# Expert layers of a streaming encoder: one gathered, sorted token table, windows copied per expert, and the scatter moved between the next gate-up matmuls

## The chip, the cores and the metric

One Trainium2 chip, one core. The metric is the device time of one launch in microseconds, the median of several runs. TensorE's clock has two levels, 1.2 and 2.4 GHz; the profile gives the granted share, 0.50 or 1.00, as PEclk.

## The reference, cut to what matters

One step of a two-layer encoder over 320 tokens (256 of a prompt, 64 of a sample). Layer 0 mixes with RWKV-7, layer 1 with windowed attention; both end in the same hierarchical mixture of experts, which is what the change touches. There are 32 experts in 4 groups; each token takes one group and two experts of it. All is float32.

```python
gu  = jnp.einsum('sd,edf->sef', t, w_gu)            # t: tokens x 1024, w_gu: 32 x 1024 x 512
hid = jax.nn.silu(gu[..., :D_EXPERT]) * gu[..., D_EXPERT:] * cw[..., None]   # D_EXPERT = 256
return jnp.einsum('sef,efd->sd', hid, w_down)       # w_down: 32 x 256 x 1024
```

`cw` is zero for every expert that a token didn't choose, so only the chosen rows need computing. A layer's expert weights are 32 x 3 MiB, 100.7 MB, all of which must come from device memory.

## The kernel before

The program is one block per engine with hand-placed semaphores. TensorE's `mm` (line 664) issues nearly all matmuls, so nearly all bear that line.

**Ahead of the expert loop** (`moe`, TensorE line 938, ScalarE 1292, VectorE 1615): mean square and normalisation (`rms`, line 1450), with the clearing of `ysum` (line 1618) between the coefficients and `rms`; router logits; the tokens turned to rows (`htok`) and split by ScalarE, GpSimd and VectorE into three bf16 parts whose sum is the float32 value (`hpart`); routing on VectorE; a rank matmul that numbers each expert's tokens (`posn`); and the number of passes, 64 slots per expert and pass.

**The expert loop** does four experts a turn, in two pairs (u = 0, 1), eight turns a pass. A pair fills the 128 rows, 64 slots for each expert:

- VectorE `select` (1719) compares `posn` with 1 to 64 and gives the one-hot matrix `sel`.
- TensorE `gather` (971): 8 chunks x 3 token tiles x 3 parts = 72 bf16 matmuls a pair, `hpart` as weights and `sel` with 128 columns as moving operand. ScalarE `gathered` (1314) copies the result to `xe`.
- TensorE turns `sel` (into `selT`) and picks the slot weights (`cwpart`).
- Gate-up, float32, 512 columns; ScalarE's SiLU (1327); VectorE's product with the slot weight (1740); `hid_turn` (985), VectorE's copy (1746); `down` (995) into banks 4 and 5.
- ScalarE, VectorE and for the first pair GpSimd (`low_parts`, 607) split the result in three bf16 parts, `dpart` (lines 1333, 1753, 1337, 1757, 618).
- The scatter: 8 chunks x 6 bf16 matmuls of 320 columns, `dpart` against `selT`; VectorE adds each chunk to `ysum` (1762).

TensorE's order in a turn is written by hand (`experts`, 1010): the selector work of both pairs, gate-up of both, first `hid_turn`, gather of the next turn's pair 0, second `hid_turn`, both `down`, gather of the next turn's pair 1, scatter. The loop is entered with both gathers of turn 0.

**The loads** are all on SyncE's queue (`moe_loads`, 485). The ring has four slots, each holding one expert's gate-up (2 MiB) and down weights (1 MiB). The slots of the first four experts are filled before the loop. In the loop, `again` (504) waits for gate-up of pair 0, issues two gate-up loads, the same for pair 1, then two down loads behind each pair's `down`.

Of the kernel before, what the change touches and what calls it, by code (L numbers as in the profile page):

```python
# [36 lines left out]
P = 128  # L37
# [19 lines left out]
TILES = [(0, 128), (128, 128), (256, 64)]  # L57
SEQS = [(0, 0, SEQ), (1, SEQ, DEC)]
# [35 lines left out]
def constants():  # L94
# [46 lines left out]
    return {"const_all": c, "const_wkv": w, "const_att": a}  # L141
# [93 lines left out]
def build(nc, i, o, known, seen):  # L235
    ctx = ExitStack()
    with ctx:
# [3 lines left out]
        def sem(name):  # L241
# [28 lines left out]
        in_sems = {n: sem(n) for n in ("const_in", "vec_in", "x_in", "wkvc_in", "attc_in", "sink_in", "cache_in",  # L270
# [3 lines left out]
            "pos_ready", "sel_ready", "selT_made", "selT_ready", "xe_made", "xe_ready",  # L274
# [51 lines left out]


        hpart = wk(3 * 3 * D // 2, BF16).rearrange("p (s j d) -> p s j d", s=3, j=3)
        ysum = wk(B).rearrange("p (c t) -> p c t", c=C)
        htok = work[:, off[0]:off[0] + 3 * D].rearrange("p (j d) -> p j d", j=3)  # L330
        xe = wk(2 * C * P).rearrange("p (u c s) -> p u c s", u=2, c=C)

        dpart = wk(3 * D, BF16).rearrange("p (u s d) -> p u s d", u=2, s=3)
        rest = wk(D).rearrange("p (n d) -> p n d", n=2)
# [4 lines left out]
        selT = wk(T, BF16).rearrange("p (u t) -> p u t", u=2)  # L339
        lg = wk(3 * 36).rearrange("p (j n) -> p j n", j=3)  # L340
# [8 lines left out]
        g48 = wk(3 * 4 * 8).rearrange("p (j g e) -> p j g e", j=3, g=4)  # L349

# [219 lines left out]
        def _(eng):  # L570
# [61 lines left out]
            eng.dma_start(cph[:, 0:AN], i["const_att"]).then_inc(in_sems["attc_in"], 16)  # L632
            split_rows(0)
# [24 lines left out]
        def _(eng):  # L658
# [279 lines left out]
            def moe(l):  # L938
# [25 lines left out]
                pe.wait("parts", l)  # L964
                pe.wait("passes", l)
# [5 lines left out]
                def gather(k, u):  # L971

                    eng.wait_ge(S["sel_ready"], 2 * k + u + 1)
                    for hf in range(2):
                        if u == 1:
                            eng.wait_ge(S["xe_ready"], 4 * k + hf + 1)
                        for cc in range(4):
                            c = 4 * hf + cc
                            for j, (t0, kt) in enumerate(TILES):
                                for n in range(3):  # L980
                                    ins = mm(ps[1 + hf][:, P * cc:P * cc + P], hpart[0:kt, n, j, P * c:P * c + P],
                                             sel[0:kt, u, j, :], j == 0 and n == 0, j == 2 and n == 2)
                        ins.then_inc(S["xe_made"], 1)

                def hid_turn(k, u):
                    eng.wait_ge(S["h_ready"], 2 * k + u + 1)
                    if u == 0:
                        eng.wait_ge(S["y_added"], 8 * k + 1)
                    else:
                        eng.wait_ge(S["hT_ready"], 2 * k + 1)  # L990
                    for f in range(2):
                        ins = eng.transpose(ps[0][:, P * f:P * f + P], hid[:, u, P * f:P * f + P], ident)  # L992
                    ins.then_inc(S["hT_made"], 1)

                def down(k, u):
                    eng.wait_ge(S["hT_ready"], 2 * k + u + 1)
                    for v in range(2):
                        eng.wait_ge(S[f"dn_in{2 * u + v}"], 16 * k + 16)
                    for n in range(2):
# [10 lines left out]
                def experts(k, e, ahead):  # L1010

                    for u in range(2):
                        eng.wait_ge(S["xe_ready"], 4 * k + 3 + u)
                        for j, (t0, kt) in enumerate(TILES):
                            mm(ps[1 + u][:, t0:t0 + kt], sel[0:kt, u, j, :], ident16[0:kt, 0:kt], True, True)

                        for j, (t0, kt) in enumerate(TILES):
                            ins = mm(ps[1 + u][:, T:T + 6].rearrange("p (s v) -> p s v", s=3), sel[0:kt, u, j, :],
                                     cwpart[0:kt, :, j, bass.ds(e + 2 * u, 2)], j == 0, j == 2)
                        ins.then_inc(S["selT_made"], 1)  # L1020
                    for u in range(2):
                        for v in range(2):
                            eng.wait_ge(S[f"gu_in{2 * u + v}"], 16 * k + 16)
                        if u == 0:
                            eng.wait_ge(S["y_added"], 8 * k)
                        for c in range(C):
                            for v in range(2):
                                ins = mm(ps[3 + 4 * u][64 * v:64 * v + 64, :], xe[:, u, c, 64 * v:64 * v + 64],
                                         w512(2 * u + v)[:, c, :], c == 0, c == C - 1)
                        ins.then_inc(S["gu_made"], 1)  # L1030
                    hid_turn(k, 0)
                    eng.wait_ge(S["selT_ready"], 2 * k + 2)
                    if ahead:
                        gather(k + 1, 0)
                    hid_turn(k, 1)
                    down(k, 0)
                    down(k, 1)
                    if ahead:
                        gather(k + 1, 1)
                    eng.wait_ge(S["hT_ready"], 2 * k + 2)  # L1040
                    for c in range(C):
                        pb = ps[(6, 7, 3, 0)[c % 4]]
# [10 lines left out]

                with eng.Fori(0, nb) as p:
                    for u in range(2):
                        gather(8 * p, u)
                    with eng.Fori(0, EXP // 4 - 1) as k_:
                        experts(8 * p + k_, 4 * k_, True)
                    experts(8 * p + 7, EXP - 4, False)
# [104 lines left out]
        def _(eng):  # L1164
# [127 lines left out]
            def moe(l):  # L1292
# [15 lines left out]
                for j, (t0, k) in enumerate(TILES):  # L1308
                    ac.wait("rest", l, j)
                    act(hpart[0:k, 1, j, :], htok[0:k, j, :], ACT.Copy, ("middle", l, j))  # L1310
                ac.wait("passes", l)
                nb = eng.value_load(passes[0:1, 2 * l:2 * l + 1], min_val=1, max_val=5)

                def gathered(k, u):
                    for hf in range(2):
                        eng.wait_ge(S["xe_made"], 4 * k + 2 * u + hf + 1)
                        eng.activation(xe[:, u, 4 * hf:4 * hf + 4, :],  # L1317
                                       ps[1 + hf][:, :].rearrange("p (c s) -> p c s", c=4),
                                       ACT.Copy).then_inc(S["xe_ready"], 1)

                def experts(k, ahead):
                    for u in range(2):
                        eng.wait_ge(S["w_ready"], 4 * k + 2 * u + 2)
                        eng.activation(selT[:, u, :], ps[1 + u][:, 0:T], ACT.Copy).then_inc(S["selT_ready"], 1)
# [3 lines left out]
                    if ahead:  # L1328
                        gathered(k + 1, 0)
                    for u in range(2):  # L1330
                        for n in range(2):
                            eng.wait_ge(S["down_made"], 4 * k + 2 * u + n + 1)
                            eng.activation(dpart[:, u, 0, 512 * n:512 * n + 512], ps[4 + n][:, :],  # L1333
                                           ACT.Copy).then_inc(S["hi_ready"], 1)
                        for n in range(2):
                            eng.wait_ge(S["rest_ready"], 4 * k + 2 * u + n + 1)
                            eng.activation(dpart[:, u, 1, 512 * n:512 * n + 512], rest[:, n, :],  # L1337
                                           ACT.Copy).then_inc(S["mid_ready"], 1)
                    if ahead:
                        gathered(k + 1, 1)  # L1340

                with eng.Fori(0, nb) as p:
                    for u in range(2):
                        gathered(8 * p, u)
                    with eng.Fori(0, EXP // 4 - 1) as k_:
                        experts(8 * p + k_, True)
                    experts(8 * p + 7, False)
# [56 lines left out]
        def _(eng):  # L1404
# [210 lines left out]
            def moe(l):  # L1615
                S = moe_sems[l]
                coefficients(f"B{l}", vcol("norm_g", 16 * l + 8, C))
                op(eng.memset(ysum[:, :, :], 0.0))
                rms(f"B{l}")
# [84 lines left out]
                op(eng.tensor_reduce(small[:, 0:1], pb[:, 96:96 + EXP], AX.X, ALU.max), ("read", "rank", l))  # L1704
                ve.settle()

# [7 lines left out]
                ve.settle()  # L1714
                eng.memset(small[:, 8:9], 0.0).then_inc(S["pos_ready"], 1)
# [3 lines left out]
                def select(e, u):  # L1719

                    for v in range(2):
                        for j, (t0, kt) in enumerate(TILES):
                            a = slice(64 * v, 64 * v + 64)
                            ins = eng.tensor_scalar(sel[0:kt, u, j, a], cst("iota", kt),
                                                    posn[0:kt, j, bass.ds(e + v, 1)], None, ALU.is_equal, ALU.bypass)
# [154 lines left out]
```

## Time and profile before

| what | value |
|---|---|
| device time, median of 3 runs | 1529.16 us (1525.72 to 1533.57) |
| the profiled execution, first to last instruction | 1526.5 us |
| TensorE matmul busy | 1355.7 us, 89% |
| VectorE busy | 521.2 us, 34% |
| ScalarE busy | 361.9 us, 24% |
| GpSimd busy | 68.4 us, 4% |
| from HBM | 293.7 MB, 194 GB/s over the span |
| gate-up loads in the page | 64, that is 32 a layer: one pass each |

A busy share over the whole span mixes stages with different limits. The two expert loops, from about 603 to 913 us and from about 1174 to 1483 us, are stages of their own and have to be read by themselves. A matmul's busy time in the rows overlaps with its neighbours', so a count times its mean is more than the time it takes; windows and timelines give the time.

### The profile page before, as it was taken

Reading aid. Unit: us, or ns where it says so; the run is one execution under the profiler, and the core shown is the slowest. Engines: PE = TensorE matmul, PEld = TensorE weight load, DVE = VectorE, ACT = ScalarE, POOL = GpSimd, SP = SyncE. Lnnn points to the kernel's source line nnn. Section 1 sums busy time; section 2 is a strip of 40 time slices with the busy share of each in tenths; the row PEclk is TensorE's granted clock in tenths of the full one; section 3 lists DMA queues with packets and bytes.
Section 4 is the critical chain, followed back from the end, with each engine's and each line's share of the span. In section 5 each row is a group of like instructions: output and inputs, shape, how many; then the busy total and the mean of one; then the engine's idle time right before and its main releaser. Section 6 shows DMA issues by size and latency. Waiting matters only on the chain.

```text
span 1526.5 us, 27571 instructions
## 1 busy us (share of the span) xinstructions
PE 1355.7 (89%) x11807; PEld 822.6 (54%) x11807; DVE 521.2 (34%) x1268; ACT 361.9 (24%) x664; POOL 68.4 (4%) x77
## 2 busy tenths in 40 slices
PE   5699998888888968999999996987968999999994
PEld 2257665565675655554444444656755555444443
DVE  2503553333312452332223235143262333222324
ACT  1131301110122022222222222134132222222212
POOL 2000000000000010000000000000010000000000
PEclk9799989998999875999999997996965999999997
DMA  9333216766734320888888845050220888888830
GB/s 272 92 111 120 100 62 244 285 234 237 276 113 165 111 83 1 331 324 299 305 304 299 305 186 184 11 205 17 83 83 1 331 330 320 302 307 298 302 121 34
DMA packets 111383, 297.16 MB, mean 195 GB/s; under 512 B 5924, under 2 KB 7304, under 8 KB 104136
## 3 DMA queue, kind: packets, MB, share of 16 engines
q1 hardware_dynamic: 109248, 289.78, 51.7%
q0 software_dynamic: 1856, 6.15, 1.7%
q8 instruction: 64, 1.05, 0.3%
q10 hardware_dynamic: 200, 0.06, 0.0%
q14 instruction: 15, 0.12, 0.0%
HBM read 293.73 MB, written 2.24 MB: 194 GB/s over the span
## 4 chain that ended last, share of the span: by engine, by line
PE 81%; DMA 8%; DVE 7%; ACT 2%; issue 1%; SPq 0%; DVEq 0%; POOL 0%; ACTq 0%; POOLq 0%
PE bank L664 79%; DMA ring<-in_ada_w 7%; DVE work L1415 3%; DMA ring<-in_kv_ada_w 1%; ACT work L1173 1%; PE bank L992 1%; DVE x_res L1421 1%; DVE work L1418 1%; DVE rstd L1453 1%; DVE att L1814 0%; PE bank L1159 0%; PE bank L1129 0%; PE bank L682 0%; SPq L450 0%; DVE work L1421 0%
## 5 line engine op out<-in xcount | busy, mean ns | idle before, releaser
L664 PE MATMUL bank<-work 128*128 128x128 bf16 (+6 forms) x3936 | 385.2, 255 | 20.0 <-ACT work L1173 7.4
L664 PEld LDWEIGHTS bank<-work 128*128 128x128 bf16 (+2 forms) x3936 | 282.1, 110 | 132.5 <-issue 30.6
L664 PE MATMUL bank<-ring,work 128*64 128x512 f32 (+1 forms) x1760 | 351.4, 553 | 1.5 <-DVE ring L1415 1.5
L664 PE MATMUL bank<-work,ring 128*128 128x320 f32 (+4 forms) x1600 | 298.9, 362 | 11.5 <-DVE work L1418 7.0
L664 PEld LDWEIGHTS bank<-work,ring 128*128 128x128 f32 (+3 forms) x1600 | 215.7, 171 | 96.2 <-issue 23.9
L664 PEld LDWEIGHTS bank<-ring,work 128*64 128x64 f32 (+1 forms) x1760 | 116.9, 138 | 214.1 <-issue 193.5
L664 PE MATMUL bank<-ring 64*64 64x64 f32 (+2 forms) x2624 | 110.7, 231 | 5.0 <-issue 5.0
L664 PEld LDWEIGHTS bank<-ring 64*64 64x64 f32 (+2 forms) x2624 | 97.5, 143 | 31.3 <-issue 25.1
L1173 ACT ACTIVATE work<-bank 64x512 f32<-64x512 f32 (+7 forms) x110 | 52.9, 528 | 226.1 <-PE bank L664 176.9
L664 PE MATMUL bank<-ring,cs 128*32 128x512 f32 x448 | 64.7, 671 | 38.6 <-DMA ring<-in_ada_w 34.4
L1762 DVE TENSOR_TENSOR work<-work,bank 128x320 f32<-128x320 f32 x128 | 62.4, 487 | 95.3 <-PE bank L664 95.3
L1173 ACT ACTIVATE ring<-bank 128x512 f32<-128x512 f32 (+4 forms) x66 | 37.3, 564 | 189.7 <-PE bank L664 188.8
L664 PE MATMUL bank<-work,const 128*128 128x320 f32 (+2 forms) x164 | 50.9, 475 | 30.1 <-DVE work L1690 17.4
L1317 ACT ACTIVATE work<-bank 128x512 f32<-128x512 f32 x64 | 38.2, 598 | 147.2 <-PE bank L664 147.2
L1753 DVE TENSOR_TENSOR work<-bank,work 128x512 f32<-128x512 f32 x64 | 44.3, 692 | 82.5 <-ACT work L1333 82.5
L618 POOL TENSOR_TENSOR work<-work 128x512 bf16<-128x512 f32 x32 | 36.4, 1159 | 648.0 <-ACT work L1337 648.0
L1746 DVE COPY work<-bank 128x256 f32<-128x256 f32 x32 | 13.6, 424 | 145.5 <-PE bank L992 145.5
L1415 DVE TENSOR_TENSOR ring<-ring,bank 128x512 f32<-128x512 f32 x45 | 29.1, 684 | 83.8 <-PE bank L664 83.7
L1327 ACT ACTIVATE work<-bank 128x256 f32<-128x256 f32 x32 | 12.3, 384 | 189.2 <-PE bank L664 189.2
L664 PEld LDWEIGHTS bank<-work,const 128*128 128x128 f32 (+1 forms) x164 | 30.4, 214 | 49.5 <-DVE work L1690 18.2
L1740 DVE SCALAR_TENSOR_TENSOR work<-work,small,bank 128x256 f32<-128x256 f32 x32 | 15.2, 475 | 120.2 <-ACT work L1327 120.2
L1333 ACT ACTIVATE work<-bank 128x512 bf16<-128x512 f32 x64 | 37.9, 593 | 62.8 <-PE bank L664 62.8
(167 smaller groups left out, 879.9 us busy)
## 6 DMA issues: line engine op xcount, KB each, us to landing
ring<-in_moe_w_gu SPq DMA_DIRECT2D x64, 2048.0 KB, 12.9
ring<-in_moe_w_down SPq DMA_DIRECT2D x64, 1024.0 KB, 12.3
ring<-in_ada_w SPq DMA_DIRECT2D x40, 1024.0 KB, 5.1
ring<-in_rw_w_rkv SPq DMA_DIRECT2D x6, 2048.0 KB, 8.0
ring<-in_ada_w SPq DMA_DIRECT2D x4, 2048.0 KB, 31.5
ring<-in_kv_ada_w SPq DMA_DIRECT2D x8, 1024.0 KB, 5.0
ring<-in_rw_w_o SPq DMA_DIRECT2D x2, 2048.0 KB, 11.7
ring<-in_at_w_q SPq DMA_DIRECT2D x2, 2048.0 KB, 14.8
```

What stands on the lines that cost most here:

```text
L618: eng.tensor_tensor(dpart[:, 0, 2, cols], rest[:, n, :], dpart[:, 0, 1, cols], ALU.subtract).then_inc(S["lo_ready0"], 1)
L664: return eng.matmul(out, l, r, start=start, stop=stop, **kw)
L992: ins = eng.transpose(ps[0][:, P * f:P * f + P], hid[:, u, P * f:P * f + P], ident)
L1173: ac.did(eng.activation(out, in_, f, **kw), *keys)
L1317: eng.activation(xe[:, u, 4 * hf:4 * hf + 4, :], ps[1 + hf][:, :].rearrange("p (c s) -> p c s", c=4), ACT.Copy).then_inc(S["xe_ready"], 1)
L1333: eng.activation(dpart[:, u, 0, 512 * n:512 * n + 512], ps[4 + n][:, :], ACT.Copy).then_inc(S["hi_ready"], 1)
L1415: op(eng.tensor_tensor(out, a, b, o_), *keys)
L1418: op(eng.tensor_scalar(out, a, s1, s2, o1, o2), *keys)
L1421: op(eng.scalar_tensor_tensor(out, a, s_, b, o1, o2), *keys)
L1453: op(eng.reciprocal(rstd[:, :], rstd[:, :]))
L1753: eng.tensor_tensor(rest[:, n, :], ps[4 + n][:, :], dpart[:, u, 0, 512 * n:512 * n + 512], ALU.subtract).then_inc(S["rest_ready"], 1)
L1762: eng.tensor_tensor(ysum[:, c, :], ysum[:, c, :], ps[(6, 7, 3, 0)[c % 4]][:, 0:T], A_).then_inc(S["y_added"], 1)
```

## The change

Each layer gathers its tokens once, ahead of the loop, into a table `xcols` that is sorted by expert: 640 columns (two experts for each of 320 tokens), and 64 columns of zero behind them. A scan over the experts' counts gives each expert's first column (`first`, and `offs` as integers). VectorE builds the one-hot matrix `selc` of 640 columns in two halves by comparing a loaded row of 1 to 640 (`iota`) with each token's two places, and TensorE multiplies in 2 x 8 x 9 matmuls of 320 columns; ScalarE evicts 16 banks. In the loop `gather` and `gathered` are gone. ScalarE reads an expert's first column into a register and copies 64 columns of the table to `xe`, once per expert (`windows`). Windows reach into the next expert's columns; those rows get a slot weight of zero and an all-zero row of `selT`.

TensorE's order in a turn becomes: gate-up of pair 0, slot weights, the scatter of the turn before, first `hid_turn`, gate-up of pair 1, `down` of pair 0, second `hid_turn`, turning of `sel`, `down` of pair 1. The last scatter stands behind the loop. Gate-up of pair 1 waits for five of the eight additions of the scatter, since they share bank 7. The `ysum` memset stands behind `rms`. `xcols` takes the place of `hT` and `htok`; `dpart` and `rest` that of `hpart`. The weight loads are unchanged. The diff, cut:

```diff
+                for hf in range(2):
+                    pe.wait("columns", l, hf)
+                    for c in range(C):
+                        pb = bank.open("xcols", l, hf, c)
+                        for j, (t0, kt) in enumerate(TILES):
+                            for n in range(3):
+                                ins = mm(pb[:, 0:T], hpart[0:kt, n, j, P * c:P * c + P],
+                                         selc[0:kt, j, T * hf:T * hf + T], j == 0 and n == 0, j == 2 and n == 2)
+                        full(ins, "xcols", l, hf, c)
-                def gather(k, u):
...
+                def experts(k, e, later):
+
+                    if later:
+                        eng.wait_ge(S["h_ready"], 2 * k - 1)
+                    gate_up(k, 0)
+                    if later:
+                        eng.wait_ge(S["selT_ready"], 2 * k)
+                    weights(k, e)
+                    if later:
+                        scatter(k - 1)
+                    hid_turn(k, 0)
+                    eng.wait_ge(S["y_added"], 8 * k - 2 if later else 8 * k + 1)
+                    gate_up(k, 1)
+                    down(k, 0)
+                    hid_turn(k, 1)
+                    turned_sel(k)
+                    down(k, 1)
...
+                for hf in range(2):
+                    for c in range(C):
+                        act(xcols[:, c, T * hf:T * hf + T], pk("xcols", l, hf, c)[:, 0:T], ACT.Copy,
+                            ("read", "xcols", l, hf, c), ("xcols ready", l))
...
+                def windows(u, e):
+
+                    at = [eng.value_load(offs[0:1, bass.ds(e + 2 * u + v, 1)], min_val=0, max_val=NA)
+                          for v in range(2)]
+                    for v in range(2):
+                        eng.activation(xe[:, u, :, 64 * v:64 * v + 64], xcols[:, :, bass.ds(at[v], SLOTS)],
                                        ACT.Copy).then_inc(S["xe_ready"], 1)
...
+                def experts(k, e_next):
                     for u in range(2):
                         eng.wait_ge(S["gu_made"], 2 * k + u + 1)
                         eng.activation(silu[:, u, :], ps[3 + 4 * u][:, 0:FE], ACT.Silu).then_inc(S["silu_ready"], 1)
+                        if e_next is not None:
+                            windows(u, e_next)
+                    parts(k, 0)
                     for u in range(2):
+                        eng.wait_ge(S["selT_made"], 2 * k + u + 1)
+                        eng.activation(selT[:, u, :], ps[1 + u][:, 0:T], ACT.Copy).then_inc(S["selT_ready"], 1)
+                    parts(k, 1)
...
                 coefficients(f"B{l}", vcol("norm_g", 16 * l + 8, C))
+                rms(f"B{l}")
                 op(eng.memset(ysum[:, :, :], 0.0))
-                rms(f"B{l}")
...
+                for hf in range(2):
+                    cols = slice(T * hf, T * hf + T)
+                    for j, (t0, kt) in enumerate(TILES):
+                        ts(selc[0:kt, j, cols], iota[0:kt, cols], place2[0:kt, 0, j:j + 1], None, ALU.is_equal,
+                           ALU.bypass)
+                    ve.settle()
+                    for j, (t0, kt) in enumerate(TILES):
+                        stt(selc[0:kt, j, cols], iota[0:kt, cols], place2[0:kt, 2, j:j + 1], selc[0:kt, j, cols],
+                            ALU.is_equal, A_, ("columns", l, hf))
```

## Rows read from the trace of the kernel before

**Rows 1.** Page, part 4: shares of the span in the chain that ended last, by line.
```profile
PE bank L664 79%; DMA ring<-in_ada_w 7%; DVE work L1415 3%; DMA ring<-in_kv_ada_w 1%; ACT work L1173 1%; PE bank L992 1%; DVE x_res L1421 1%; DVE work L1418 1%; DVE rstd L1453 1%; DVE att L1814 0%; PE bank L1159 0%; PE bank L1129 0%; PE bank L682 0%; SPq L450 0%; DVE work L1421 0%
```

**Rows 2.** Windows: us, busy us (instructions) per engine, PEclk, DMA share, GB/s.
```profile
603.30:912.99 309.69, 308.73 (x2229) 152.68 (x2228) 89.86 (x247) 81.79 (x135) 18.12 (x16) 0.99 0.77 286
...
653.78:694.41 40.63, 40.63 (x306) 20.74 (x304) 12.26 (x34) 11.17 (x19) 2.27 (x2) 1.00 0.82 310
```

**Rows 3.** Timeline of one turn: start, us, engine, line, operation, count.
```profile
620.02 5.75 PE L664 MATMUL bank<-work 128*128 128x128 bf16 x72
...
633.09 13.47 PE L664 MATMUL bank<-work 128*128 128x128 bf16 x132
...
646.48 13.96 PE L664 MATMUL bank<-ring,work 128*64 128x512 f32 x64
...
653.78 10.09 SPq L476 DMA_DIRECT2D ring<-in_moe_w_gu  x4
```

**Rows 4.** Windows of one turn's loads.
```profile
653.78:656.32 2.54, 2.54 (x14) 0.87 (x12) 2.18 (x12) 0.22 (x1) 0.00 (x0) 1.00 0.39 130
...
656.32:658.86 2.54, 2.54 (x14) 0.87 (x12) 0.24 (x2) 0.00 (x0) 0.00 (x0) 1.00 1.00 359
...
656.32:676.64 20.32, 20.32 (x166) 9.92 (x163) 5.54 (x11) 6.15 (x11) 2.27 (x2) 1.00 1.04 385
...
676.64:686.80 10.16, 10.16 (x93) 7.22 (x93) 4.05 (x9) 2.48 (x3) 0.00 (x0) 1.00 1.03 409
```

**Rows 5.** Timeline ahead of the first layer's expert loop.
```profile
503.07 0.37 SPq L481 DMA_DIRECT2D ring<-in_moe_w_down  x1
...
541.34 2.19 DVE L1618 MEMSET work<- 128x2560 f32 x1 [0.60 <-DVE coef L1415]
...
579.51 0.18 DVE L1704 TENSOR_REDUCE small<-bank 128x1 f32<-128x32 f32 x1
...
581.46 1.28 ACT L1317 ACT_TABLE_LOAD   x1 [6.25 <-DVE passes L1713]
...
581.52 0.06 DVE L1717 MEMSET small<- 128x1 f32 x1 [0.89 <-issue]
...
582.81 20.57 PE L664 MATMUL bank<-work 128*128 128x128 bf16 x156 [3.74 <-DVE work L1724]
```

**Rows 6.** Windows in which the granted clock is low or rises.
```profile
582.81:603.30 20.49, 20.49 (x156) 13.65 (x156) 1.24 (x8) 3.17 (x5) 0.00 (x0) 0.50 0.00 1
...
603.30:613.16 9.86, 9.86 (x35) 3.02 (x36) 0.32 (x2) 2.71 (x5) 0.00 (x0) 0.74 0.00 0
...
915.10:919.42 4.32, 4.32 (x20) 2.53 (x21) 1.62 (x4) 0.00 (x0) 0.00 (x0) 0.60 1.04 386
...
919.42:923.46 4.04, 4.03 (x30) 2.67 (x28) 2.43 (x5) 0.00 (x0) 0.00 (x0) 1.00 1.05 387
```

**Rows 7.** Timeline of TensorE, the last scatter of the layer.
```profile
915.10 8.36 PE L664 MATMUL bank<-work 128*128 128x320 bf16 x48 [2.11 <-DVE work L1757]
```

**Rows 8.** Groups by line and shape: busy, mean ns of one, idle before.
```profile
L1753 DVE TENSOR_TENSOR work<-bank,work 128x512 f32<-128x512 f32 x64 | 44.3, 692 | 82.5 <-ACT work L1333 82.5
...
L1333 ACT ACTIVATE work<-bank 128x512 bf16<-128x512 f32 x64 | 37.9, 593 | 62.8 <-PE bank L664 62.8
...
L1421 DVE SCALAR_TENSOR_TENSOR work<-work,vec 128x320 f32<-128x320 f32 x56 | 27.1, 547 | 57.8 <-PE bank L664 57.5
...
L1746 DVE COPY work<-bank 128x256 f32<-128x256 f32 x32 | 13.6, 424 | 145.5 <-PE bank L992 145.5
...
L1327 ACT ACTIVATE work<-bank 128x256 f32<-128x256 f32 x32 | 12.3, 384 | 189.2 <-PE bank L664 189.2
```

**Rows 9.** Timeline, three single pieces, two of TensorE and one of VectorE.
```profile
236.20 1.06 PE L664 MATMUL bank<-ring,cs 128*32 128x512 f32 x8 [0.25 <-DMA ring<-in_ada_w]
...
239.98 1.93 PE L664 MATMUL bank<-ring,cs 128*32 128x512 f32 x8 [2.71 <-DMA ring<-in_ada_w]
...
1512.10 2.46 DVE L1418 TENSOR_SCALAR work<-work,vec 128x320 f32<-128x320 f32 x8
```

More of the change, by code:

```diff
@@ L632, in _ @@
             eng.dma_start(cph[:, 0:AN], i["const_att"]).then_inc(in_sems["attc_in"], 16)
+            pl.wait("y rstd all", C - 1)
+            eng.dma_start(iota, i["const_iota"].broadcast_to([P, NA])).then_inc(in_sems["iota_in"], 16)
             split_rows(0)
@@ L969, in moe, with weights @@
                 nb = eng.value_load(passes[0:1, 2 * l:2 * l + 1], min_val=1, max_val=5)
-                def gather(k, u):
[L973 to L983, printed above, removed]
+                def weights(k, e):
+                    eng.wait_ge(S["sel_ready"], k + 1)
+                    for u in range(2):
+                        for j, (t0, kt) in enumerate(TILES):
+                            ins = mm(ps[1 + u][:, T:T + 6].rearrange("p (s v) -> p s v", s=3), sel[0:kt, u, j, :],
+                                     cwpart[0:kt, :, j, bass.ds(e + 2 * u, 2)], j == 0, j == 2)
+                    ins.then_inc(S["w_made"], 1)
@@ L1008, in down, with scatter @@
                         ins.then_inc(S["down_made"], 1)
[L1010 to L1031, printed above, removed]
-                    eng.wait_ge(S["selT_ready"], 2 * k + 2)
[L1033 to L1040, printed above, removed]
+                def scatter(k):
+                    eng.wait_ge(S["selT_ready"], 2 * k + 2)
                     for c in range(C):
-                        pb = ps[(6, 7, 3, 0)[c % 4]]
+                        pb = ps[(7, 6, 4, 5)[c % 4]]
                         if c % 4 == 0:
@@ L1052, in experts @@
                         ins.then_inc(S["y_made"], 1)
+                def experts(k, e, later):
[14 more added lines that the diff above has]
+                    down(k, 1)
                 with eng.Fori(0, nb) as p:
-                    for u in range(2):
-                        gather(8 * p, u)
-                    with eng.Fori(0, EXP // 4 - 1) as k_:
+                    experts(8 * p, 0, False)
+                    with eng.Fori(1, EXP // 4) as k_:
                         experts(8 * p + k_, 4 * k_, True)
-                    experts(8 * p + 7, EXP - 4, False)
+                    scatter(8 * p + 7)
                 pe.wait("x moe", l)
@@ L1714, in moe @@
                 ve.settle()
+                ve.wait("xcols ready", l)
                 eng.memset(small[:, 8:9], 0.0).then_inc(S["pos_ready"], 1)
@@ new lines, in remainder, with added @@
+                def remainder(k, u, n):
+                    eng.wait_ge(S["hi_ready"], 4 * k + 2 * u + n + 1)
+                    if u == 1:
+                        eng.wait_ge(S["lo_ready0"], 2 * k + n + 1)
+                    eng.tensor_tensor(rest[:, n, :], ps[4 + n][:, :], dpart[:, u, 0, 512 * n:512 * n + 512],
+                                      ALU.subtract).then_inc(S["rest_ready"], 1)
+                def added(k):
+                    for c in range(C):
+                        eng.wait_ge(S["y_made"], 8 * k + c + 1)
+                        eng.tensor_tensor(ysum[:, c, :], ysum[:, c, :], ps[(7, 6, 4, 5)[c % 4]][:, 0:T],
+                                          A_).then_inc(S["y_added"], 1)
@@ L1729, in experts @@
+                def experts(k, e_next, later):
+                    eng.wait_ge(S["w_made"], k + 1)
                     for u in range(2):
-                        eng.wait_ge(S["selT_made"], 2 * k + u + 1)
                         for v in range(2):
```

185 lines of the change are left out of this document (113 added, 72 removed).

## The prediction

> **What bounds the kernel now.** I read the chain that ended last first. It names TensorE's generic matmul line for 79% of the span [rows 1]. Then I cut the expert loop of each layer into its turns (one turn handles four experts). Each turn takes 40.63 us, the TensorE column is as long as the window, and the granted clock is 1.00, so nothing there waits for a load; the turns of the other layer are the same [rows 2]. From the start of the first gate-up to the end of the last down projection a layer takes 309.7 us [rows 2]. TensorE's own timeline then shows what fills a turn [rows 3]: gate-up 13.9 us, transposes of the hidden rows 0.7, the gather of the first pair for the next turn 5.7 (72 matmuls; the row's 5.75 runs into the next), down 7.0, and a block of 132 bf16 matmuls of 13.4 that holds the second gather, the scatter and twelve small ones. Last I read the DMA side of a turn [rows 4]: 12.58 MB, at 385 GB/s while gate-up weights move and 409 GB/s while down weights move, busy share above 1; over the whole turn the share is 0.82 [rows 2], so some 7 us of it nothing moves. The reader is to see two limits: TensorE at 40.63 us, and right under it the transfers, at 8.39 MB / 385 GB/s + 4.19 MB / 409 GB/s = 21.8 + 10.2 = 32.0 us. A shorter TensorE turn meets the second one.
>
> **Part 1, the gathers leave the loop.** The block of 132 holds 72 gathers and 48 scatter matmuls; those run at 4.04 us for 30 at full clock [rows 6], 0.135 us each, 6.5 us; the rest, 6.9 us for 84 matmuls, is 0.08 us each, so the second gather is 5.7 us. TensorE's work per turn becomes 40.63 - 5.7 - 5.7 = 29.2 us.
>
> **Part 2, the scatter is moved.** Today the second gather is the cover under which ScalarE, VectorE and GpSimd split the down result. The last turn has no such gather, and there TensorE stands 2.11 us before the scatter and then runs it at a lower clock [rows 6, 7]. Without the move every turn would pay that. Moved behind the next gate-up (6.9 us, longer than the 2.11 us) it costs nothing. What comes late next is the second down: on ScalarE the split of the first down now queues behind a SiLU, two register reads and two copies. SiLU 0.4 and 0.1 to start, reads 0.9 each, copies 0.6 each, then eviction 0.6, remainder 0.7 and the transposed copy 0.45 [rows 8] is 5.2 us after gate-up, when TensorE is there after 3.5 + 0.3 + 0.75 = 4.6 us. So a stall of 0.6 us, a turn of 29.8 us. The register reads are not in the loop today; the nearest row is VectorE's, where 0.89 us pass between two memsets around one read [rows 5]. I take 0.9, with 0.1 (the gap was VectorE's own and not the read's; no stall) and twice the row, 1.8, as the ends. The copies themselves (128x512 elements) answer to the 0.60 us eviction of the same size [rows 8]; they replace it one for one.
>
> **Part 3, the transfers take the turn.** The loads are the same and SP issues them on the same releases, gate-up slots behind gate-up, down slots behind down. With TensorE at 29.8 and the transfers at 32.0 us the queue always holds the next load: its pair-0 gate-up load is released some 10 us before the queue reaches it, the pair-1 load likewise, the down loads over 20 us before. So there is no pause, and the turn is 32.0 us. Counted from the start of the first gate-up: 9.9 us to its end, at the clock of today [rows 6]; 1.7 us to the first bytes (issue at 653.78, and 130 GB/s in that window is 0.85 us of moving) [rows 4]; six turns of 32.0; 10.9 for the gate-up weights of the last turn's first pair; then the whole of TensorE's turn, 29.2. Sum 9.9 + 1.7 + 192.0 + 10.9 + 29.2 = 243.7 us. TensorE alone would need 27.7 for the first turn (9.9 for its first gate-up, no scatter, and 1.3 in which VectorE weighs the rows) and 7 x 29.8, 236.3 us, so the transfers add 7 us. Saved: 309.7 - 243.7 = 66.0 us a layer. After it the tail (2.11 and 8.36 us of scatter) is today's [rows 7]. TensorE now waits about 2 us a turn. Such a wait of 2.11 us is followed by half clock in the last scatter, one of 2.71 us doubles eight matmuls from 1.06 to 1.93 us [rows 6, 7, 9]. That costs about 2 us when it happens, which fills the wait and prevents the next one, so I price it at 0, with +2 a layer as its upper end.
>
> The Trainium skill (DMA: Bandwidth & Descriptors, section Where 436 GB/s comes from) says that for transfers from HBM the per-core HBM share of about 358 GB/s binds. The trace disagrees: 385 to 409 GB/s over 30 us [rows 4].
>
> **Part 4, the table before the loop.** VectorE: counts, a scan, first places, offsets and the two places are eight dependent small steps of 0.16 to 0.26 us with gaps, some 2.0 us; then half the columns' one-hot matrix, three compares of 0.31 [rows 9] and three compare-adds of 0.55 at 320 columns [rows 8], 2.6 us. From 579.5 us that ends at 584.2, against 582.81 where the gather starts now [rows 5]: +1.4. The other half runs beside TensorE. TensorE: 2 x 8 x 9 = 144 matmuls of 320 columns. At full clock one is 0.135 us (above), at half clock 0.267 (320 columns / 1.2 GHz). The clock is 0.50 before it. The same shape rises from 0.60 to 1.00 within 4.3 us [rows 6], so 144 x 0.135 + 2.3 (4.3 us at half do the work of 2.1) = 21.8 us, against 20.5 for what it replaces [rows 5]: +1.3. If the clock stays at half it is 38.4. Handover, in which today's first gate-up waits for nothing: last eviction 0.5, ScalarE's register read 0.9, table load 1.28 [rows 5], a small copy 0.2, two reads 1.8, two copies 1.2: +5.9, ends +3 and +9. The memset of 128x2560 (2.19 us) goes from before the mean square's result, where it is hidden, to behind the reciprocal and ahead of the normalisation that waits for VectorE [rows 5]: +2.1. The constant's load on GpSimd's queue is released by the same event as SP's down load at 503 us and wanted near 582 [rows 5]. Nothing for it. Together 1.4 + 1.3 + 5.9 + 2.1 = +10.7 us a layer.
>
> **Sum.** -66.0 + 10.7 = -55.3 us a layer, -110.6 for two. From the profiled span of 1526.5 that is 1415.9; the median of the runs is 2.7 above that span, so **1419 us**. Its own range is 1404 to 1436.
>
> **Rivals.**
> (A) The clock stays at half through the table's 144 matmuls. For it: the 156 matmuls there now are busy for 20.5 us at a granted clock of 0.50 and never rise [rows 6]. Against it: those have 128 columns, and both the 320-column scatter and the 512-column gate-up rise. Price 38.4 - 21.8 = 16.6 a layer, 1452 us. Chance 0.13. The Trainium skill (TensorE: Matmul & The Clock Gate, section What's actually happening) says that sustained work brings the full clock; by that, A is out. The present gathers, at half clock for all of their 20.5 us, speak against it here, which is why A keeps its chance.
> (B) The memory rate is lower once the loads stream without the pause. The lowest full window of a burst has 359 GB/s, its first [rows 4]; nothing falls off towards the end. At 359 throughout a turn is 35.0 us: 6 x 3.0 and 0.8 more for the last load make +18.8 a layer, 1457 us. Chance 0.04. The rate that the skill's DMA page says binds would give the same time.
> (C) ScalarE's chain sets the turn. With 1.8 us a read, the second down stands 2.4 us, TensorE's turn is 31.6 and the layer's loop 27.7 + 7 x 31.6 = 248.9; with 1.8 more in the handover +7.0 a layer, 1433 us. Chance 0.07.
> (D) The transfers run at 409 GB/s throughout or better, TensorE's 236.3 us holds: -7.4 a layer, 1404 us. Chance 0.06.
> (E) Slower: each turn's wait for weights drops the clock, and it doesn't come back in the turn. The profile has such drops after waits of 2.1 and 2.7 us [rows 7, 9]. TensorE's turn at half clock is 29.8 + some 29 = 59 us, the layer over 450 instead of 309.7, the kernel about 1840 us. It decides from the point where the half clock takes back 55 us a layer, 7.9 us a turn beyond 32.0: 39.9 us of turn, 20 of them at half clock. Against it: the scatter is back at 1.00 after 4.3 us and gate-up within 5.2 [rows 6]. Chance 0.04. The skill's clock page (section HAM oscillation — how this bites in real kernels) describes just this pattern, a DMA wait in each step and a cold start of the next; by it a turn would lose what one such drop costs, the 2 us above, and not the whole turn.
> (F) A second pass over the experts, in which the change would double the copies: the page counts 64 gate-up loads, one pass a layer, and routing is not changed. No chance given.
>
> **How the numbers follow.** Forecast 0.66, A 0.13, B 0.04, C 0.07, D 0.06, E 0.04. C and D lie inside or at the edge of the forecast's range. The 80% range reaches down to 1400 (handover +3, rates of 409) and up to 1455, to take in A. A measurement of this kernel tells some 0.5% from no change. Faster by more than that: all but E, 0.94; same 0.01; slower 0.05.
>
> **What would show it.** Right: turns of about 32 us, DMA share near 1 through the loop, TensorE waiting about 2 us a turn for the gate-up weights, first gate-up some 11 us later than now. A shows as 0.50 in the table's stretch; B as under 370 GB/s; C as a longer stall before the second down with DMA pauses; D as turns under 31 us; E as a mean clock under 0.8 in the loop. The prediction is wrong if the turn is over 34 us or the stretch from rank to first gate-up is over 40 us at full clock.

## The result and the profile after

The changed kernel takes 1427.47 us (median of 6 runs, 1419.94 to 1432.04) against 1528.72 us for the kernel before (6 runs): ratio 0.9328, 95% interval 0.9292 to 0.9364. The profiled execution has a span of 1418.4 us; before, 1526.5. The forecast was 1419 us, 1404 to 1436 in its own range, 1400 to 1455 in all.

The page names a second owner of the chain that ended last, the gate-up loads of the expert loop, with 19%; before, no load of expert weights was in that chain [rows 1]. Page of the changed kernel, part 4, shares of the span by engine and by line:

```profile
PE 58%; DMA 29%; DVE 8%; ACT 2%; issue 1%; SPq 1%; ACTq 0%; DVEq 0%; POOL 0%; POOLq 0%
PE bank L676 57%; DMA ring<-in_moe_w_gu 19%; DMA ring<-in_ada_w 8%; DVE work L1447 3%; ACT work L1197 2%; DMA ring<-in_kv_ada_w 1%; DVE work L1450 1%; DVE x_res L1453 1%; DVE rstd L1485 1%; DVE att L1898 0%; SPq L486 0%; DVE work L1453 0%; PE bank L1153 0%; DVE work L1651 0%; SPq L460 0%
```

(`mm` is line 676 now, `op`'s helpers moved by 32.) The windows show why. The first is the loop from first gate-up to last down of layer 0, the next two a turn in each layer, cut at SP's down loads; columns as in rows 2:

```profile
614.40:859.36 244.96, 234.37 (x1232) 101.05 (x1232) 100.31 (x250) 72.95 (x130) 18.18 (x16) 0.98 0.96 364
...
698.75:730.68 31.93, 29.51 (x156) 13.01 (x154) 12.03 (x33) 8.26 (x14) 0.69 (x1) 0.95 1.04 394
...
1214.41:1246.33 31.92, 29.50 (x156) 12.95 (x154) 12.02 (x34) 8.18 (x15) 0.59 (x2) 0.95 1.04 394
```

A turn went from 40.63 to 31.93 us. Its DMA share is 1.04 where it was 0.82, at 394 GB/s, and TensorE is no longer busy for all of it. The wait is where it was looked for, ahead of a turn's first gate-up. TensorE's timeline in layer 0, three such places:

```profile
702.18 8.78 PE L676 MATMUL bank<-ring,work 128*64 128x512 f32 x32 [2.42 <-DMA ring<-in_moe_w_gu]
...
734.09 7.09 PE L676 MATMUL bank<-ring,work 128*64 128x512 f32 x32 [0.73 <-DMA ring<-in_moe_w_gu]
...
766.03 7.09 PE L676 MATMUL bank<-ring,work 128*64 128x512 f32 x32 [2.45 <-DMA ring<-in_moe_w_gu]
```

The 32 records take 7.09 us, or 8.78 where the clock had dropped. The wait after such a slow one is only 0.73 us: the lost time comes out of the next wait. And a wait of 2.45 us left the clock alone once where one of 2.42 us didn't.

The stretch ahead of the loop, which grew, in one timeline (layer 0):

```profile
540.20 2.15 DVE L1485 RECIPROCAL rstd<-rstd 128x320 f32<-128x320 f32 x1 [0.54 <-ACT rstd L1197]
542.83 2.19 DVE L1651 MEMSET work<- 128x2560 f32 x1 [0.48 <-issue]
545.06 2.89 DVE L1447 TENSOR_TENSOR work<-x_res,rstd 128x960 f32<-128x960 f32 x2
...
577.55 0.18 DVE L1736 COPY work<-bank 128x32 f32<-128x32 f32 x1
...
582.34 28.31 PE L676 MATMUL bank<-work 128*128 128x320 bf16 x144 [5.24 <-DVE work L1453]
...
614.40 8.78 PE L676 MATMUL bank<-ring,work 128*64 128x512 f32 x32 [3.75 <-ACT work L1347]
```

The memset lies between reciprocal and normalisation. The table takes 28.31 us, and the first gate-up comes 3.75 us behind it. In three windows the table's clock:

```profile
582.34:590.00 7.66, 7.66 (x27) 3.02 (x27) 3.26 (x14) 0.87 (x2) 0.00 (x0) 0.50 0.00 0
590.00:595.00 5.00, 5.00 (x21) 2.09 (x21) 0.00 (x0) 0.93 (x3) 0.00 (x0) 0.60 0.00 0
595.00:610.65 15.65, 15.65 (x99) 7.68 (x97) 0.00 (x0) 4.75 (x11) 0.00 (x0) 1.00 0.00 1
```

27 matmuls in 7.66 us at half clock, 99 in 15.65 at full: 0.158 us each there, where I had 0.135. In layer 0 the granted clock is 0.50 for the first 11.7 us of the table, in layer 1 for the first 4.0.

**The sum, term by term**, in us. Each layer is taken from SP's last load ahead of it (539.50 and 1109.79 before, 534.78 and 1054.53 after) to the end of its last scatter.

| term | forecast | layer 0 | layer 1 |
|---|---|---|---|
| memset on the path | +2.1 | +2.8 | +2.5 |
| VectorE ahead of the table | +1.4 | +1.5 | +1.8 |
| table instead of first gathers (20.5) | +1.3 | +7.8 | +4.3 |
| handover to the first gate-up | +5.9 | +3.7 | +3.5 |
| loop (309.7, 309.6) | -66.0 | -64.7 | -64.6 |
| last scatter (8.36, 8.35) | 0 | -1.7 | -1.7 |
| sum, as measured whole | -55.3 | -50.6 | -54.2 |

So 105 of the 108 us between the two profiled executions are in the two layers, where 110.6 were forecast. The rest, -3.3, is -4.7 ahead of layer 0, in code that the change doesn't touch, and +1.4 elsewhere.

### The profile page after: what moved, and what is told of

Same layout as the page of the kernel before. It is cut to its first block, busy times and chain, and to the rows that moved or that the text cites. A ratio compares the mean times of both kernels' runs of the same rounds, so it can differ in the third digit from the quotient of the medians.

```text
span 1418.4 us, 23836 instructions
## 1 busy us (share of the span) xinstructions
PE 1213.2 (86%) x9791; PEld 713.8 (50%) x9791; DVE 555.7 (39%) x1316; ACT 353.9 (25%) x685; POOL 68.9 (5%) x78
## 4 chain that ended last, share of the span: by engine, by line
PE 58%; DMA 29%; DVE 8%; ACT 2%; issue 1%; SPq 1%; ACTq 0%; DVEq 0%; POOL 0%; POOLq 0%
PE bank L676 57%; DMA ring<-in_moe_w_gu 19%; DMA ring<-in_ada_w 8%; DVE work L1447 3%; ACT work L1197 2%; DMA ring<-in_kv_ada_w 1%; DVE work L1450 1%; DVE x_res L1453 1%; DVE rstd L1485 1%; DVE att L1898 0%; SPq L486 0%; DVE work L1453 0%; PE bank L1153 0%; DVE work L1651 0%; SPq L460 0%
## 5 line engine op out<-in xcount | busy, mean ns | idle before, releaser
L676 PE MATMUL bank<-ring,work 128*64 128x512 f32 (+1 forms) x1760 | 359.4, 560 | 27.5 <-DMA ring<-in_moe_w_gu 18.8
L676 PE MATMUL bank<-work 128*128 128x320 bf16 (+9 forms) x1920 | 237.8, 291 | 23.2 <-DVE work L1453 10.5
L676 PEld LDWEIGHTS bank<-ring,work 128*64 128x64 f32 (+1 forms) x1760 | 124.5, 139 | 241.0 <-issue 237.4
L676 PEld LDWEIGHTS bank<-work 128*128 128x128 bf16 (+2 forms) x1920 | 165.2, 119 | 103.4 <-issue 37.9
L1197 ACT ACTIVATE work<-bank 128x320 f32<-128x320 f32 (+7 forms) x142 | 66.2, 509 | 279.8 <-PE bank L676 232.2
L676 PE MATMUL bank<-ring 64*64 64x64 f32 (+2 forms) x2624 | 110.6, 231 | 4.4 <-issue 4.3
L676 PE MATMUL bank<-work,const 128*128 128x320 f32 (+2 forms) x164 | 53.4, 492 | 31.4 <-DVE work L1722 18.1
L1784 DVE TENSOR_SCALAR work<-const,work 128x64 bf16<-128x64 f32 (+1 forms) x192 | 57.8, 372 | 0.2
L1823 DVE TENSOR_REDUCE small<-bank 64x1 f32<-64x3 f32 x64 | 10.1, 158 | 107.4 <-PE bank L676 105.9
L1453 DVE SCALAR_TENSOR_TENSOR work<-work,vec 128x320 f32<-128x320 f32 x56 | 27.1, 546 | 57.8 <-PE bank L676 57.5
## 6 DMA issues: line engine op xcount, KB each, us to landing
ring<-in_moe_w_down SPq DMA_DIRECT2D x64, 1024.0 KB, 15.8
```

The costliest lines, as they stand in the source:

```text
L676: return eng.matmul(out, l, r, start=start, stop=stop, **kw)
L1197: ac.did(eng.activation(out, in_, f, **kw), *keys)
L1453: op(eng.scalar_tensor_tensor(out, a, s_, b, o1, o2), *keys)
```

## The experiments

All edits are to the changed kernel. Times are compared with its own: 1427.5 us for the first four experiments, and 1423.5 in a second set of runs for the others. The first four experiments ran in a set in which the kernel before took 1525.11 us, against 1528.72 beside the changed kernel; by the ratios to it the differences given below for the shorter loads, the scatter, and the two sizes of added work would be -29, +55, +9 and +39 us instead of -33, +47, +2 and +35. So the loops in the traces decide: from the first gate-up to the end of the last down of layer 0 it is 244.96 us in the changed kernel, and 233.5, 268.8, 246.3 and 263.3 in these four.

**Shorter loads.** Is it the transfers that set the turn? Each gate-up load in the loop brings half of its bytes, so the kernel leaves out half of those weights.

```diff
 with again(): for v in range(2):
-    moe_gu(l, 2 * u + v, e + 2 * u + v)
+    s = 2 * u + v
+    eng.dma_start(slot(s, 2048)..., i["moe_w_gu"][l, bass.ds(e + s, 1), 0:512]...)
```

> The changed kernel with each gate-up reload cut to its first half of rows (1 MiB instead of 2; the other half of the slot keeps older weights, so the computation uses wrong weights there). A turn then moves 8.39 MB instead of 12.58, about 21 us of transfers. Theory 1, the transfers set the turn: the waits for gate-up weights vanish and the turn falls from 31.93 to TensorE's own 29.35 us; from first gate-up to last down 26.0 + 7 x 29.35 = 231.4 us instead of 245.0, so 13.5 us a layer and 27 us in all less than the changed kernel. Rival, the turn is set by TensorE's chain of waits on the other engines and the DMA waits are incidental: the turn stays within 0.5 us of 31.9 and the time within 8 us.

Measured 1394.52 us (1390.98 to 1398.04), 33 less, ratio to before 0.9137 (0.9098 to 0.9175). A turn's window:

```profile
683.21:712.48 29.27, 29.27 (x162) 12.80 (x162) 13.70 (x34) 9.67 (x18) 2.27 (x2) 1.00 0.77 285
```

29.27 us, TensorE busy throughout, clock 1.00, DMA share 0.77. Theory 1 holds; the transfers cost 2.66 us a turn. The loop took 233.5 us against 231.4 expected: its first turn had a clock drop that the changed kernel's didn't have, 1.7 us, and a first gate-up of 9.6 us, 0.9 longer. The two loops account for 23 us, as against 29 or 33 in the medians. It also shows TensorE's chain bare: 29.27 us against 29.2 of work, so the 0.6 us stall before the second down, which I had put in, isn't there.

**More TensorE work in each turn**, twice, to find the knee:

```diff
-                    for f in range(2):
+                    for f in [0, 1] * (7 if u == 0 else 1):      # 12 more; 19 for 36 more
                         ins = eng.transpose(ps[0][:, P * f:P * f + P], hid[:, u, P * f:P * f + P], ident)
```

> The changed kernel with 12 more transposes of the same hidden rows in each turn, about 2.0 us of TensorE work, ahead of the second gate-up. Theory 1, the transfers set the turn: TensorE's turn becomes 31.4 us, still below 31.93, so the turn stays and only the last turn, which is counted whole, grows: 2 us a layer, 4 us in all. Rival, TensorE sets the turn: 2.0 us in 8 turns of 2 layers, 32 us more, turns of 33.9 us.

> The same with 36 more transposes, about 6.1 us a turn. Theory 1 (the turn is the larger of TensorE's and the transfers'): TensorE's turn is 35.5 us and now sets the pace, no waits for weights; first gate-up to last down 26.0 + 6.1 + 7 x 35.5 = 280.6 us instead of 245.0, 71 us more in all. Rival, the two costs add up (waits stay as they are): 6.1 x 8 x 2 = 98 us more, turns of 38 us.

Measured 1429.91 us (1428.07 to 1434.91) and 1462.11 (1453.92 to 1465.02), 2 and 35 us more. The windows, an early and a late turn of the first, one of the second:

```profile
649.75:680.32 30.57, 30.57 (x174) 14.08 (x174) 13.80 (x34) 9.67 (x18) 2.27 (x2) 1.00 1.04 393
774.17:806.09 31.92, 30.80 (x174) 14.38 (x174) 13.80 (x34) 9.67 (x18) 2.28 (x2) 1.00 1.04 394
```

```profile
689.47:722.67 33.20, 33.20 (x198) 16.73 (x198) 13.79 (x34) 9.67 (x18) 2.27 (x2) 1.00 1.01 380
```

A transpose cost 0.109 us (1.30 / 12 and 3.93 / 36; TensorE's own rows say the same, 1.69 us for 14 transposes and 4.31 for 38 where 2 take 0.38), not the 0.17 that I had taken. So the first experiment added 1.3 us a turn and not 2.0, the second 3.9 and not 6.1, and the 71 us expected of it were twice too many. With that price the rule of the larger one holds at both points: 29.27 + 1.30 = 30.57 is TensorE's turn, hidden under 31.92 once the queue sets the pace; 29.27 + 3.93 = 33.20 is above it and shows whole. A sum of both costs would have been 35.9. The early turn of 30.57 us shows the other half of the mechanism: the first turn's weights are in the ring already, and TensorE starts ahead of the queue. The turns of layer 0 begin at 649.75, 680.32, 710.90, 742.25 and 774.17 us: two at its own pace of 30.6, one of 31.35, and from then on the queue's 31.92. The loop grew by only 1.3 us with the first size, 10.4 us of work in eight turns. With the second, 31.4 us of work, it grew by 18.3 to 263.3, near the 264.9 that the bare chain of the shortened loads gives with this work added (233.5 + 31.4); that chain's first turn had the clock drop of 1.7 us, and this one's hadn't.

**The scatter back at the end of its turn.** What is the move worth by itself?

```diff
                     weights(k, e)
-                    if later:
-                        scatter(k - 1)
                     hid_turn(k, 0)
-                    eng.wait_ge(S["y_added"], 8 * k - 2 if later else 8 * k + 1)
+                    eng.wait_ge(S["y_added"], 8 * k + 1)
                     gate_up(k, 1)
                     down(k, 0)
                     hid_turn(k, 1)
                     turned_sel(k)
                     down(k, 1)
+                    scatter(k)
```

> The changed kernel with the scatter put back to the end of its own turn, no gather there to cover it. Theory 1, the transfers hide most of it: TensorE's turn is 29.35 plus the 2.11 us stand before the scatter, plus up to 1.7 where the clock drops, 31.5 to 33.2 us, beside 32 us of transfers; so turns of 32 to 33.2 us, 0 to 9 us a layer, 0 to 18 us in all more. Rival, moving the scatter earns its whole price: 2.11 + 1.7 in each of 7 turns of both layers, 53 us more, turns of 35.7 us.

Measured 1474.58 us (1464.64 to 1483.18), 47 more, ratio to before 0.9688 (0.9637 to 0.9739). Theory 1 allowed 18 us at most and is out. The time is near the rival's 53, but not by its mechanism. TensorE's timeline:

```profile
707.74 6.68 PE L676 MATMUL bank<-work 128*128 128x320 bf16 x48 [2.70 <-DVE work L1837]
714.35 7.09 PE L676 MATMUL bank<-ring,work 128*64 128x512 f32 x32
...
723.26 0.44 PE L1025 MATMUL bank<-const,work 128*128 128x128 f32 x2 [1.34 <-DVE work L1792]
723.63 12.22 PE L676 MATMUL bank<-ring,work 128*64 128x512 f32 x48
...
743.17 8.36 PE L676 MATMUL bank<-work 128*128 128x320 bf16 x48 [2.71 <-DVE work L1837]
```

and the windows of an undisturbed turn and of this one:

```profile
654.19:687.91 33.72, 29.68 (x162) 12.57 (x162) 13.88 (x34) 9.67 (x18) 2.27 (x2) 1.00 1.01 379
721.64:758.75 37.11, 33.06 (x162) 13.58 (x162) 13.89 (x34) 9.68 (x18) 2.28 (x2) 0.91 0.93 341
```

There are two stands, not one: 2.70 us before the scatter for the split, and 1.34 us before the first `hid_turn`, in which VectorE reduces the slot weights and multiplies them in. The moved scatter covers both. TensorE's turn is 33.7 us, 4.4 more than without them, of which the transfers hide 2.66. And each stand can drop the clock: in this turn twice, 1.7 us each time, 37.1 in all. The loop takes 268.8 us instead of 245.0. That is seven turns of 33.7, the 26.0 that the expectations count for the first, and four drops of 1.7 us: with the stands, TensorE's chain sets every turn, and the transfers none.

**The memset later**, where VectorE waits for the logits:

```diff
                 rms(f"B{l}")
-                op(eng.memset(ysum[:, :, :], 0.0))
                 ve.settle()
                 normed(f"B{l}", hT)
                 modulated(f"B{l}", hT, hT, range(C - ACT_CHUNKS))
+                op(eng.memset(ysum[:, :, :], 0.0))
```

> The changed kernel with the clearing of ysum (2.19 us) moved behind VectorE's share of the modulation, where TensorE's router logits keep VectorE waiting 8.7 us. Theory: in the changed kernel the memset lies whole on the path, with 0.5 us of waiting on its own engine, so 2.7 us a layer and 5 us in all less than the changed kernel; in the trace the normalisation starts right behind the reciprocal. Rival: the path there is TensorE's or ScalarE's and the memset costs nothing, no change in the distance from reciprocal to logits.

Measured 1419.21 us (1417.39 to 1423.20) beside 1423.52 (1421.76 to 1434.69) for the changed kernel in the same set, 4 us less. The ranges of the whole times overlap, the stage decides:

```profile
547.38 2.15 DVE L1485 RECIPROCAL rstd<-rstd 128x320 f32<-128x320 f32 x1 [0.54 <-ACT rstd L1197]
549.56 2.89 DVE L1447 TENSOR_TENSOR work<-x_res,rstd 128x960 f32<-128x960 f32 x2
...
555.92 2.19 DVE L1654 MEMSET work<- 128x2560 f32 x1 [0.60 <-DVE work L1450]
```

From the reciprocal's start to the normalisation's it is 2.18 us instead of 4.86: 2.7 us a layer, as expected. It reaches the table: from SP's last load to the table's first matmul it is 44.9 us in layer 0, 47.6 in the unedited kernel beside it.

**Work ahead of the table**, in TensorE's 5.2 us of waiting:

```diff
                 full(ins, "rank", l)
+                pb = bank.open("warm1", l)
+                for _w in range(3):
+                    ins = mm(pb[:, :], cst("ones"), const[:, 0:512], True, True)
+                full(ins, "warm1", l)
+                seen.at[("read", "warm1", l)] = seen.at[("warm1", l)]
                 pe.wait("parts", l)
```

> The changed kernel with three float32 matmuls of 512 columns, whose result nobody reads, behind the rank matmuls, in the 5.2 us in which TensorE waits for the first half of the one-hot matrix. Theory 1: the table's matmuls take 28.3 and 24.8 us instead of 22.9 (144 x 0.159 at full clock) because the clock is at half for their first 11 and 5 us; with work in the wait it is up near their start, 23 to 24.5 us, 1 to 5 us a layer and 2 to 9 us in all less. Rival: the clock doesn't rise on such work ahead either, the table takes as long as in the changed kernel and the time is the same or, where the dummy work overruns the wait, up to 3 us more.

Measured 1420.43 us (1416.63 to 1424.99), 3 less than the changed kernel beside it, in ranges that overlap. The table decides:

```profile
580.74 4.45 PE L676 MATMUL bank<-const 128*128 128x512 f32 x6
586.12 22.96 PE L676 MATMUL bank<-work 128*128 128x320 bf16 x144 [0.93 <-DVE work L1458]
```

22.96 us in both layers, 144 x 0.159, at a granted clock of 1.00 throughout, where the unedited kernel in the same set took 26.80 and 24.80. Theory 1: what the table took above 22.9 us was the clock. How long the clock stays down isn't a property of the layer alone: without this work ahead, seven profiled executions took between 24.7 and 28.3 us in layer 0 and between 24.8 and 26.0 in layer 1.

**Both, and work ahead of the logits too** (seven such matmuls behind `mean_square`):

> Both of these together, and seven such matmuls also between the mean square and the router logits, where TensorE stands about 7 us and then runs the 48 logit records of 36 columns in 10.9 us at a granted clock of 0.50. Theory: the logits start at full clock; they are bound by their weight loads and not by their columns, so I expect 6 to 8 us instead of 10.9; with the memset 2.7 and the table 1 to 5 that is 7 to 12 us a layer, 14 to 24 us in all less than the changed kernel, 1403 to 1413 us. Rival: the logits are bound by issue and gain nothing, 1412 to 1420 us.

Measured 1414.87 us (1412.27 to 1422.07), ratio to before 0.9263 (0.9211 to 0.9314): 9 us less than the changed kernel beside it, the fastest median that computes the whole. That misses what was expected, 1403 to 1413 us or 14 to 24 less, and lies in the rival's range of 1412 to 1420. But the logits did gain, so the rival's reason is out too. The logits of layer 0, whole and in two parts:

```profile
554.03 8.21 PE L676 MATMUL bank<-router,work 128*128 128x36 f32 x48 [1.03 <-DVE work L1460]
...
554.03:557.00 2.97, 2.97 (x23) 2.66 (x23) 2.37 (x9) 0.06 (x1) 0.00 (x0) 1.00 0.00 0
557.00:562.24 5.24, 5.24 (x28) 4.66 (x28) 2.06 (x3) 0.00 (x0) 0.00 (x0) 0.58 0.01 3
```

8.21 us, and 8.86 in layer 1, instead of 10.92, a mean clock of 0.73 in the first. The clock that the matmuls ahead had kept up was 1.00 for the first 3 us and then lost again within the 36-column matmuls. So this part brought 2.7 and 2.1 us, where 3 to 5 were expected. From SP's last load ahead of a layer to its first reload it is 78.0 us in both layers, 88.0 and 84.6 in the unedited kernel: 17 us in the stages, against 9 in the medians and 7 in the profiled spans (1413.0 and 1420.0). In the profiled pair 6.4 of the 10 us between 17 and 7 lie ahead of layer 0, in code that is the same in both: SP's last load there came at 542.72 us with the edit and at 536.28 without. Another 3.1 were lost between layer 0's first reload and layer 1; the last scatter of layer 0 had a clock drop with the edit (8.36 us, 6.68 without). Whether the medians hide part of the gain in the same way, I can't tell from these runs.

**The changed kernel again:**

> The changed kernel itself, unedited, beside the other three on one chip. Expected: 1427 us within 6 us, the spread of its six runs, so that differences of the other three under 5 us are read from stages of their traces and not from the whole time.

Measured 1423.52 us (1421.76 to 1434.69), ratio 0.9334 (0.9277 to 0.9390), the same as the first time.

## Why the prediction was right

**What bounds, and what would bound next.** Right, and shown by the shortened loads and by the two sizes of added work: a turn is the larger of TensorE's chain and the transfers. The transfers' price, 32.0 us from two windows of a kernel in which they had pauses, was 31.93 [rows 4]. Rival B, a lower rate in a continuous stream, is out: 394 GB/s. So are D, whose faster transfers didn't come, and E: the mean clock of the loop is 0.98, and the drop costs 1.7 us, out of a wait. E's price was also added wrongly: its own terms, 27.7 + 7 x 59, make 441 us a layer and some 1814 in all, not over 450 and 1840. F is out as well, the page still counts 64 gate-up loads.

**Part 1 and the loop's sum.** 243.7 us forecast, 245.0 measured in both layers. TensorE's work of 29.2 us was right. The stall before the second down was not there, since ScalarE's register reads are 0.5 us each: 0.99 us lie between SiLU and the first of two copies. ScalarE's timeline of the changed kernel:

```profile
647.43 0.38 ACT L1363 ACTIVATE work<-bank 128x256 f32<-128x256 f32 x1 [3.18 <-PE bank L676]
648.80 1.16 ACT L1347 ACTIVATE work<-work 128x512 f32 x2 [0.99 <-issue]
```

By the prediction's own sum, 0.8 us less on ScalarE brings it ahead of TensorE. Rival C had the reads at 1.8 and is out. This error was harmless only because the transfers hid it.

**Part 2.** The direction was right, the price too small: I counted the 2.11 us stand of the old last turn [rows 7] and not the chain through VectorE behind the slot weights, though I had put its 1.3 us into the first turn. By the experiment the move is worth 4.4 us of TensorE's turn, plus clock drops, 23.8 us a layer in all. Without the move the change would have brought half of what it did, 51 us (against 1525.11 us for the kernel before, measured beside it) and not 101.

**Part 4.** Forecast +10.7 us a layer, measured +15.8 in layer 0 and +12.1 in layer 1, 6.5 more in all. The term that was mis-sized is the table's, "144 x 0.135 + 2.3". Its first part is too small in both layers: 22.9 us at full clock (144 x 0.159, as the work ahead of the table showed) and not 19.4. Nine matmuls of the table take 1.43 us and not 1.22. The scatter's matmuls, from which I took the 0.135, all have 128 rows; the table's third token tile has 64, and of every nine three are of that tile. TensorE's weight-load timeline of the changed kernel, at full clock, in the table and then in a scatter (start, busy, and the idle time before each group):

```profile
600.56 0.66 PEld L676 LDWEIGHTS bank<-work 128*128 128x128 bf16 x6 [0.26 <-issue]
601.48 0.25 PEld L676 LDWEIGHTS bank<-work 64*128 64x128 bf16 x3 [0.26 <-issue]
...
862.01 2.54 PEld L676 LDWEIGHTS bank<-work 128*128 128x128 bf16 x19
```

Each change between 64 and 128 rows has a gap of 0.26 us ahead of it, and the scatter's loads have none. The single matmul records of the same trace tell that it is the change and not the smaller tile. At full clock the table's matmuls start 0.14 us apart within a group, be it of 64 or of 128 rows, and 0.23 us apart at a change of rows; the scatter's start 0.136 us apart throughout. Two changes in nine matmuls are the missing 0.2 us. The kernel before has the same steps in its gathers, 0.06 us within a group and 0.15 at a change, so the 0.08 us of Part 1 holds the changes and the 0.135 doesn't. That the change of rows costs this was read from the records and not tried in an experiment.

The second part, what the low clock costs, was too small in layer 0 only: 5.4 us against 2.3, and 1.9 in layer 1. There the clock rose after 11.7 and 4.0 us. So the table cost 28.3 and 24.8 instead of 21.8 us. Layer 0 had a part of what rival A describes, 3.1 us of its price of 16.6; layer 1 had none. Why the clock rose late in layer 0 stays open.

Against it stand the handover, 3.7 and 3.5 instead of 5.9 us, and the last scatter, in which no drop came in either layer. In the handover the single read takes 0.5 us and not 0.9, and the two reads ahead of the window copies leave no gap at all. The missing drop is luck: behind the same wait of 2.1 us the last scatter took 8.3 us in both layers of the run with 12 more transposes. That the two layers together came within 5.8 us of the forecast is in part such cancelling: the table was 9.5 us over, the handovers 4.6 and the scatters 3.4 us under.

**The base.** I took the offset from span to median, 2.7 us, from one kernel. The profiled execution of the changed kernel lasted 1420.17 us, 1.8 above its span and near the lowest of its six, so from its span to the median it is 9.1 us. Of the 8.9 us between the forecast and the median, 5.8 are the two layers and 3.1 are this base: 6.4 more in the offset, 3.3 less in the code outside the layers. Much of the spread seems to come from a part that the change leaves alone, as the last point below shows.

## What to carry to other kernels

When an engine is busy for the whole of a loop turn, price the next limit in the same turn from its own bursts before counting a saving: here 11.4 us of removed matmuls became 8.7, and bytes over burst rate gave the new turn to 0.1 us. When work is moved, list every stand that it covers today and would cover tomorrow, on each engine's chain; the scatter covered two, and one was missed. Take a matmul's price from one with the same rows in the weight tile and the same clock history, not only the same columns.

## What the runs showed of the hardware that I had not expected

- A granted clock of 0.50 lasted 20.5 us under busy 128-column gathers [rows 6], and 11.7 and 4.0 us under the 320-column table. The full clock that had been kept up for the 36-column logits was lost 3 us into them.
- A wait of 2.42 us dropped the clock, one of 2.45 didn't, at the same place of two turns. In the loop the drop cost 1.7 us. Behind a wait of 2.11 us the last scatter took 6.68 us in one run and 8.35 in another.
- A register read on ScalarE costs about 0.5 us when two follow each other, against 0.89 us for a single one on VectorE [rows 5]; at the same place of layer 1 VectorE's took 0.63.
- Changing between weight tiles of 64 and 128 rows goes with about 0.1 us each time: at full clock 0.23 us from start to start at the change against 0.14 beside it with 320 columns, 0.15 against 0.06 with 128. Nine matmuls of 320 columns take 1.43 us with two changes, 1.22 without.
- Executions differ ahead of layer 0: in nine executions of kernels whose code is the same up to there, SP's last load before it is issued between 534.8 and 542.7 us. That is of the size of most of the 12 us between the fastest and the slowest run of the changed kernel; that it is the same spread wasn't shown, since no kernel was profiled more than twice.
